# First weight unit of a fused two-block transformer kernel: token loads cut anew, rounding spread over four engines, products reordered

## The reference, cut to what matters

```
h    = concatenate([meta_tokens, x])                  # 528 x 1024
xn   = h * rsqrt(mean(h*h) + 1e-6) * norm_gains[0]
proj = xn @ w_in                                      # q, k, v, forget, gates
```

## Time and profile before

| | us |
|---|---|
| median of 3 runs | 2178.06 |
| lowest, highest | 2177.88, 2178.19 |
| profiled execution, its own time | 2178.15 |
| its span, first to last instruction | 2176.4 |
| PE busy in the span | 2141.2 |
| first product of the unit stream starts | 9.38 |
| sum of squares (after unit 0 and half of unit 1) starts | 29.75 |

### The profile page before, as it was taken

How to read it: one execution, slowest core, us unless ns; L and a number is a source line. 1 busy time by engine, 2 the same in 40 slices (tenths; PEclk the granted TensorE clock), 3 DMA queues, 4 the chain that set the end, 5 groups by cost and what they waited for, 6 DMA issues and landing times.

```text
span 2176.4 us, 31347 instructions
## 1 busy us (share of the span) xinstructions
PE 2141.2 (98%) x12490; PEld 1845.6 (85%) x12490; DVE 996.5 (46%) x1460; ACT 755.3 (35%) x1017; POOL 1008.2 (46%) x825
## 2 busy tenths in 40 slices
PE   8999999999999999999999999999999999999998
PEld 7897999999999887888888788878788888888886
DVE  5144454379888207322200829671876442222027
ACT  4133455243222216322212415551336332222134
POOL 4322223455555547555544545254331555555444
PEclk9999999999999999999999999999999999999999
DMA  4322112212222323322222221114220222222222
GB/s 165 103 69 69 59 45 73 97 59 97 96 85 89 108 96 109 122 96 96 97 97 96 98 105 43 58 58 155 78 78 21 97 97 97 96 96 97 96 100 94
DMA packets 31950, 195.17 MB, mean 90 GB/s; under 512 B 3968, under 2 KB 4480, under 8 KB 10096
## 3 DMA queue, kind: packets, MB, share of 16 engines
q1 hardware_dynamic: 26352, 182.66, 23.4%
q10 hardware_dynamic: 5504, 11.18, 1.7%
HBM read 189.47 MB, written 4.23 MB: 89 GB/s over the span
## 4 chain that ended last, share of the span: by engine, by line
PE 79%; issue 8%; POOL 5%; DVE 5%; ACT 1%; DMA 0%; SPq 0%; DVEq 0%; POOLq 0%; ACTq 0%
PE ps L2370 69%; POOL wlo L708 5%; PE ps L2965 2%; DVE sqa L1520 1%; PE ps L3180 1%; PE ps L3164 1%; PE ps L3047 1%; DVE x2lo L1508 1%; PE ps L3100 1%; PE ps L2649 1%; PE ps L2672 0%; PE ps L3145 0%; PE ps L2708 0%; DMA h<-h 0%; PE ps L3190 0%
## 5 line engine op out<-in xcount | busy, mean ns | idle before, releaser
L708 POOL TENSOR_TENSOR wlo<-raw,whi 128x512 fp32r<-128x512 f32 (+2 forms) x820 | 1006.8, 1260 | 1142.6 <-ACT whi L774 1038.4
L774 ACT CAST whi<-raw 128x2048 fp32r<-128x2048 f32 x162 | 309.6, 1911 | 809.2 <-PE ps L2370 751.9
L2370 PE MATMUL ps<-x2hi,whi 128*128 128x512 f32 x1136 | 448.6, 395 | 1.2 <-DVE x2lo L1508 1.1
L2370 PE MATMUL ps<-x2hi,wlo 128*128 128x512 f32 x1136 | 442.4, 389 | 0.0
L2370 PE MATMUL ps<-x2lo,whi 128*128 128x512 f32 x1136 | 442.2, 389 | 0.0
L2370 PE MATMUL ps<-xhi,whi 128*128 128x256 f32 (+2 forms) x1336 | 270.7, 284 | 15.2 <-DVE xlo L1574 9.4
L2370 PE MATMUL ps<-xlo,whi 128*128 128x256 f32 (+2 forms) x1336 | 268.0, 282 | 0.0
L2370 PE MATMUL ps<-xhi,wlo 128*128 128x256 f32 (+2 forms) x1336 | 268.0, 282 | 0.0
L2370 PEld LDWEIGHTS ps<-x2hi,whi 128*128 128x128 f32 x1136 | 213.3, 188 | 49.6 <-issue 4.8
L2370 PEld LDWEIGHTS ps<-x2hi,wlo 128*128 128x128 f32 x1136 | 213.3, 188 | 44.7
L2370 PEld LDWEIGHTS ps<-x2lo,whi 128*128 128x128 f32 x1136 | 213.4, 188 | 44.4 <-issue 1.7
(11 more groups left out here) (471 smaller groups left out, 2759.8 us busy)
## 6 DMA issues: line engine op xcount, KB each, us to landing
raw<-wstream SPq DMA_DIRECT2D x170, 1024.0 KB, 4.8
h<-h SPq DMA_DIRECT2D x4, 528.0 KB, 8.7
ncb<-c_rows ACTq DMA_DIRECT2D x8, 256.0 KB, 3.4
ple_rows<-ple_out ACTq DMA_DIRECT2D x4, 512.0 KB, 4.1
bias<-bias_rows ACTq DMA_DIRECT2D x8, 256.0 KB, 4.8
ple<-ple_rows ACTq DMA_DIRECT2D x4, 512.0 KB, 5.5
out_dram<-outb SPq DMA_DIRECT2D x8, 256.0 KB, 2.8
raw<-wstream ACTq DMA_DIRECT2D x4, 256.0 KB, 7.3
```

Source lines behind the costliest of these rows:

```text
L708: return nc.gpsimd.tensor_tensor(wlo[b][:, cols], raw[b][:, cols], whi[b][:, cols].bitcast(F32), ALU.subtract)
L774: nc.scalar.copy(whi[b][:], raw[b][:]).then_inc(sig("hi_done"), 1)
L2370: ins = mm(dst, w[slot][:, cols], xx(tok), start=first and p_ == 0, stop=last and p_ == 2, skip_group_check=True)
```

## The change

The gains of the first norm and eight columns of zeros are put in front of the tokens in the same rows (`hg`, 16 + 8 x 528 columns), so the first token transfer brings the gains. SP loads the tokens in five pieces of 1, 1, 1, 2 and 3 chunks, then unit 1, then the three small constants. ACT loads unit 0 as two quarters and a half, and `cv` behind them, and loads its function table ahead of its first wait.

The rounding of unit 0 is spread: ACT rounds quarter 0 and all of `xhi`, POOL copies quarters 1 to 3 to `whi`, DVE makes the four quarters of `wlo` between its eight `xlo`. Unit 1 is rounded by ACT in four quarters, POOL makes its low part, and PE waits for it by quarters.

PE first runs ten products of a zeroed tile (256 columns, fp32) into a bank that is not yet in use, waits for quarter 0, and runs one more. Then it goes over k with the high x high products of chunk k ahead of the other two of chunk k-1.

The diff, cut to its core:

```diff
+HG = 16
...
-    h0 = np.ascontiguousarray(tokens.T.reshape(KC, P, T1).transpose(1, 0, 2))
+    h0 = tokens.T.reshape(KC, P, T1).transpose(1, 0, 2).reshape(P, KC * T1)
+    h0 = np.concatenate([columns(v["norm_gains"][0][0]), np.zeros((P, HG - KC), np.float32), h0], axis=1)
...
-        h = at("h", [P, KC, T1])
+        hg = at("hg", [P, HG + KC * T1])
+        h = hg[:, HG:].rearrange("p (k t) -> p k t", t=T1)
+        x_loads = [(0, 1), (1, 2), (2, 3), (3, 5), (5, KC)]
...
+        idle = at("idle", [P, HALF], offset=arena)
...
-        QUARTERED = [0, U_UP + 1, U_UP + 2, U_PLEP, U_F1I, U_F1I + 1, U_F1I + 2, U_PLEG + 3]
+        QUARTERED = [0, 1, U_UP + 1, U_UP + 2, U_PLEP, U_F1I, U_F1I + 1, U_F1I + 2, U_PLEG + 3]
...
-        HI_FIRST = [0, U_UP + 1, U_UP + 2, U_F1I + 1]
+        HI_FIRST = [0, 1, U_UP + 1, U_UP + 2, U_F1I + 1]
...
-            sp.dma_start(cv[:], cvec).then_inc(sig("gains_in"), 16)
-            for q in range(4):
-                sp.dma_start(h[:, 2 * q:2 * q + 2, :], h0[:, 2 * q:2 * q + 2, :]).then_inc(sig(f"h_in{q}"), 16)
+            for n, (a, z) in enumerate(x_loads):
+                cols = slice(HG + a * T1 if a else 0, HG + z * T1)
+                sp.dma_start(hg[:, cols], h0[:, cols]).then_inc(sig("part_in3" if n == 4 else f"h_in{n}"), 16)
...
+            sp.dma_start(fw0[:], fw).then_inc(sig("consts_in"), 16)
+            sp.dma_start(ident[:], ident_c).then_inc(sig("consts_in"), 16)
+            sp.dma_start(masks[:], masks_c).then_inc(sig("consts_in"), 16)
...
+            for q in range(1, 4):
+                cols = slice(q * BANK, (q + 1) * BANK)
+                if q < 3:
+                    pool.wait_ge(sig(f"part_in{q}"), 16)
+                pool.wait_ge(sig("hi_first"), q)
+                nc.gpsimd.tensor_copy(whi[0][:, cols], raw[0][:, cols]).then_inc(sig("hi_first" if q < 3 else "hi_done"), 1)
+            pool.wait_ge(sig("lo_done"), 1)
...
-                    pool.wait_ge(sig("hi_first"), q + 1)
-                    low_part(0, q).then_inc(sig("lo_first"), 1)
+                    pool.wait_ge(sig("hi_first"), 3 + q + 1)
+                    low_part(1, q).then_inc(sig("lo_first"), 1)
...
-                    pool.wait_ge(sig("hi_done"), 1)
-                    low_part(0, q).then_inc(sig("lo_done"), 1)
-            pool.wait_ge(sig("hi_done"), 2)
-            for q in range(3):
-                low_part(1, q)
-            low_part(1, 3).then_inc(sig("lo_done"), 1)
+                    pool.wait_ge(sig("hi_done"), 2)
+                    low_part(1, q).then_inc(sig("lo_done"), 1)
...
+            act.dma_start(raw[0][:, 0:BANK], wstream[0][:, 0:BANK]).then_inc(sig("part_in0"), 16)
+            act.dma_start(raw[0][:, BANK:2 * BANK], wstream[0][:, BANK:2 * BANK]).then_inc(sig("part_in1"), 16)
+            act.dma_start(raw[0][:, 2 * BANK:], wstream[0][:, 2 * BANK:]).then_inc(sig("part_in2"), 16)
+            act.dma_start(cv[:], cvec).then_inc(sig("gains_in"), 16)
+            nc.scalar.preload_act_table_set("natural_log_exp_and_others")
+            act.wait_ge(sig("part_in0"), 16)
+            nc.scalar.copy(whi[0][:, 0:BANK], raw[0][:, 0:BANK]).then_inc(sig("hi_first"), 1)
+            for n, (a, z) in enumerate(x_loads):
+                act.wait_ge(sig("part_in3" if n == 4 else f"h_in{n}"), 16)
+                for k in range(a, z):
+                    nc.scalar.activation(xhi[:, k, :], h[:, k, :], ACT.Copy, scale=hg[:, k:k + 1]
+                                         ).then_inc(sig("xhi_ready"), 1)
+            act.wait_ge(sig("hi_done"), 1)
+            act.wait_ge(sig("raw_ready1"), 16)
+            act.wait_ge(sig("hi_first"), 3)
...
-                act.dma_start(raw[0][:, q * BANK:(q + 1) * BANK], wstream[0][:, q * BANK:(q + 1) * BANK]
-                              ).then_inc(sig(f"part_in{q}"), 16)
-            act.dma_start(fw0[:], fw).then_inc(sig("fw_in"), 16)
-            act.dma_start(ident[:], ident_c).then_inc(sig("ident_in"), 16)
-            act.dma_start(masks[:], masks_c).then_inc(sig("masks_in"), 16)
-            act.wait_ge(sig("gains_in"), 16)
-            for q in range(4):
-                act.wait_ge(sig(f"part_in{q}"), 16)
...
-                nc.scalar.copy(whi[0][:, cols], raw[0][:, cols]).then_inc(sig("hi_first" if q < 3 else "hi_done"), 1)
-                act.wait_ge(sig(f"h_in{q}"), 16)
-                for k in (2 * q, 2 * q + 1):
-                    nc.scalar.activation(xhi[:, k, :], h[:, k, :], ACT.Copy, scale=cv[:, G_PRE + k:G_PRE + k + 1]
-                                         ).then_inc(sig("xhi_ready"), 1)
-            hi_of(1)
-            nc.scalar.preload_act_table_set("natural_log_exp_and_others")
+                nc.scalar.copy(whi[1][:, cols], raw[1][:, cols]).then_inc(sig("hi_first" if q < 3 else "hi_done"), 1)
...
-            act.wait_ge(sig("fw_in"), 16)
+            act.wait_ge(sig("consts_in"), 48)
+            act.wait_ge(sig("gains_in"), 16)
...
-            act.wait_ge(sig("ident_in"), 16)
-            act.wait_ge(sig("masks_in"), 16)
...
+            vec.memset(idle[:], 0.0).then_inc(sig("cols_ready"), 1)
...
-            dve.wait_ge(sig("gains_in"), 16)
...
+                if k % 2 == 0:
+                    q, cols = k // 2, slice(k * HALF, k * HALF + BANK)
+                    dve.wait_ge(sig("hi_first" if q < 3 else "hi_done"), q + 1 if q < 3 else 1)
+                    vec.tensor_tensor(wlo[0][:, cols], raw[0][:, cols], whi[0][:, cols].bitcast(F32), ALU.subtract
+                                      ).then_inc(sig("lo_first" if q < 3 else "lo_done"), 1)
...
-                vec.scalar_tensor_tensor(out=xlo[:, k, :], in0=h[:, k, :], scalar=cv[:, G_PRE + k:G_PRE + k + 1],
+                vec.scalar_tensor_tensor(out=xlo[:, k, :], in0=h[:, k, :], scalar=hg[:, k:k + 1],
...
+            dve.wait_ge(sig("gains_in"), 16)
...
+            def idle_turns(n):
+                for _ in range(n):
+                    mm(bank(7)[:, 0:HALF], idle[:, 0:P], idle[:], start=True, stop=True)
+            def high_tile(k, c):
+                for dst, tok in wide_places(STAGE1[c]):
+                    ins = mm(dst, whi[0][:, (2 * k + c) * P:(2 * k + c + 1) * P], xhi[:, k, tok], start=k == 0,
+                             stop=False, skip_group_check=True)
+                return ins
+            def low_tile(k, c):
+                cols = slice((2 * k + c) * P, (2 * k + c + 1) * P)
+                for w, xx, last in ((whi, xlo, False), (wlo, xhi, k == KC - 1)):
+                    for dst, tok in wide_places(STAGE1[c]):
+                        ins = mm(dst, w[0][:, cols], xx[:, k, tok], start=False, stop=last, skip_group_check=True)
+                return ins
+            pe.wait_ge(sig("cols_ready"), 1)
+            idle_turns(10)
+            pe.wait_ge(sig("hi_first"), 1)
+            idle_turns(1)
+            for k in range(KC + 1):
+                if k < KC:
+                    if k % 2 == 0:
+                        pe.wait_ge(sig("hi_first" if k < 6 else "hi_done"), k // 2 + 1 if k < 6 else 1)
+                    pe.wait_ge(sig("xhi_ready"), k + 1)
+                    for c in range(2):
+                        high_tile(k, c)
+                if k >= 1:
+                    if k % 2 == 1:
+                        low_ready(0, k // 2)
+                    pe.wait_ge(sig("x_ready"), k)
+                    for c in range(2):
+                        ins = low_tile(k - 1, c)
+                        if k == KC:
+                            ins.then_inc(sig("unit_done" if c else "half"), 1)
...
-                    if k < 6:
-                        pe.wait_ge(sig("lo_first"), k // 2 + 1)
-                    else:
-                        pe.wait_ge(sig("lo_done"), 1)
-                pe.wait_ge(sig("x_ready"), k + 1)
-                ins = chunk_tile(0, 0, k, STAGE1[0])
-                if k == KC - 1:
-                    ins.then_inc(sig("half"), 1)
-                ins = chunk_tile(0, 1, k, STAGE1[1])
-            ins.then_inc(sig("unit_done"), 1)
-            pe.wait_ge(sig("lo_done"), 2)
-            chunk(1, 0, 2)
-            pe.wait_ge(sig("cols_ready"), 1)
+                    low_ready(1, k // 2)
+                ins = chunk_tile(1, 0, k, STAGE1[2])
+            ins.then_inc(sig("half"), 1)
+            pe.wait_ge(sig("cols_ready"), 2)
```

## The result

| | before | after |
|---|---|---|
| median, us | 2177.97 (4 runs, 2177.88 to 2178.19) | 2190.97 (4 runs, 2190.36 to 2192.56) |
| ratio of times | | 1.0061 (95% interval 1.0049 to 1.0073) |
| span of the profiled execution, us | 2176.4 | 2188.7 |
| sum of squares starts, us | 29.75 | 26.54 |
| from there to the end, us | 2146.61 | 2162.16 |

The change made the kernel 13.0 us slower, where 3.8 us faster was forecast. The last two lines say where: up to the sum of squares 3.2 us were gained, and behind it, in code that the change does not touch, 15.5 us were lost.

What follows compares the result with a forecast made beforehand. PE, busy 98% of the span, was taken as the bound; 1.5 us by earlier S, 2.0 by the clock and 0.62 by the gap, less 0.5 of stalls, gave 3.8 us gained: 2174.3 us, range 2173.3 to 2176.6.

Steps and rivals of the forecast that it cites:

- Everything behind 29.75: All work from the sum of squares on: taken to move along whole, so its start, 29.75 us before, measures the change.
- the last, that later stages lose: Rival, behind the start: the start moves and later stages wait for something else instead; chance 0.04.
- S = 7.86: Start of PE's first real product, after idle products from 1.17 us: 4.0 us slow, then 2.69 us fast.
- Idle products of zeros don't raise the clock: Rival, PE's start: idle work leaves the clock slow, S = 10.55, kernel at 2178.4 us; chance 0.06.
- The fast pace: PE's early products: 0.122 us each at 2.4 GHz, 17.57 us for unit 0 and unit 1's first chunk.
- Landings: Token transfers at the start: chunk 2 lands at 9.32 us, chunks 3 and 4 at 10.96, chunks 5 to 7 at 12.9.
- Small pieces: Rival, first transfers: small pieces come at 291 GB/s, 2.9 us gained, kernel at 2175.1 us; chance 0.12.
- ACT's table load ahead of the wait: ACT's start: the 1.28 us table load is hidden behind the transfer, ending near 4.1 us.
- POOL copy, 1.3 us: POOL's copies of unit 0's quarters 1 to 3: 1.3 us each, hidden even at 1.85.
- DVE as the bound: Rival, unit 0's low parts: DVE slowed beside POOL ends 1.6 us late, kernel at 2175.9 us; chance 0.10.
- The squares, 0 to 0.3 us late: DVE's adds of squares ahead of the sum: end near 25.3 to 26.2, wanted at 25.94; taken as 0.
- 2.0 us by the clock: PE's first real products: 2.0 us gained because idle products raise the clock before them.

Runs made afterwards that it cites:

- b1_pad64: The kernel before with 64 unused bytes behind the tokens and no instruction changed: 2193.17 us, ratio 1.0069 to the kernel before.
- a_gap256: The changed kernel with 192 more unused bytes behind the tokens, 256 bytes of added distance in all: 2174.99 us, ratio 0.9988 to the kernel before.
- a_gap512: The changed kernel with 448 more unused bytes behind the tokens, 512 bytes of added distance in all: 2175.47 us, ratio 0.9989 to the kernel before.
- best_x0: `a_gap256` in the old product order, with output-stage and first feed-forward inputs 0 instead of 8 columns into their rows: 2177.86 us, ratio 1.0000 to before.
- a_noidle: `a_gap256` without its eleven idle products: 2175.37 us, ratio 0.9988 to the kernel before.
- a2_tail64: The changed kernel with 64 unused bytes behind the tokens, everything behind them 128 bytes further than before the change: 2211.22 us, ratio 1.0157 to before.

## Why the prediction was wrong

The step that failed is the one the sum rested on: "Everything behind 29.75 is released by PE's own progress or by ACT and DVE steps that start from it. I take it to move along whole". The releases did move along whole. What I did not ask is whether the work behind keeps its pace. It did not: 64 bytes more ahead of the token-side buffers cost 2.2 ns on each product of 512 columns and somewhat on shorter ones, 15.5 us together (`b1_pad64`: 15.4 alone). The kernel has some 6000 products of 512 columns, by estimate 13 of the 15.5 us; the products of 256 and 258 columns have most of the rest. The edit that did it stood in the diff as a layout detail, `hg` in place of `h`, and I priced it at nothing without naming it. None of the rivals had it; the last, that later stages lose, was there with a chance of 0.04 and the wrong mechanism.

The rest, point by point:

- *S = 7.86.* Real products began at 8.10. The idle pitch halved 4.7 us after the first idle product, not 4.0; in `a_gap256` 6.0 us after, and S was 8.74. The term was right in kind and 0.2 to 0.9 us too small.
- *Idle products of zeros don't raise the clock.* They do: records 427 ns apart turn into records 216 ns apart before any real product has run.
- *The fast pace.* 0.122 us a product stood beside a row that gives 4.0/34 = 0.118, because the row counts products cut by the window's edges too. After the change a pair takes 0.243 us in the timeline, so 0.122 was right.
- *Landings.* The count of bytes that must come first gave 9.32, 10.96 and 12.9; ACT could start at 9.58, 11.22 and 13.13. Small pieces were not slow.
- *ACT's table load ahead of the wait.* It lies at 3.11 to 4.39, hidden.
- *POOL copy, 1.3 us.* It took 0.87 and hid as forecast:

```profile
L724 POOL CAST whi<-raw 128x512 fp32r<-128x512 f32 x3 | 2.6, 874 | 8.5 <-DMA raw<-wstream 8.5
```

- *DVE as the bound.* No: its last `xlo` of unit 0 ended at 16.7.
- *The squares, 0 to 0.3 us late.* 0.16 us in the changed kernel, 0 (`a_gap512`) to 0.61 (`best_x0`) in those at 256 or 512 bytes.
- *2.0 us by the clock.* This was no gain on top of the earlier inputs. `a_noidle` has the slow start still and its median is 0.4 us above that of `a_gap256`, less than the runs can tell; in the profiles its sum of squares starts 0.1 us behind that of `a_gap256` and 0.8 behind that of the changed kernel. With the tokens as late as they are, the two terms overlap; my sum counted them apart and took only 0.5 us of stalls off.
- *The start in sum.* 3.8 us forecast, 3.2 measured, and 2.9 at the end of the kernel once the distance is a multiple of 256 bytes again.

## What to carry to other kernels

Ask of every edit which buffers it moves, and compare the pitch of an untouched product deep in the kernel before anything else: a count of products in one window that PE fills shows in a minute what no list of waits does. When a buffer grows, keep the distance between the matrices loaded as weights and those that move past them at the multiple of 256 bytes it had, here by 192 unused bytes. That is shown for fp32r products of 512 columns only; for pairs of 256 and 258 columns it was not the best place. A gain of some us at the start is lost easily to a percent of pace behind it.

## What the runs showed of the hardware

- The pace of an fp32r product of 512 columns depends on the distance, modulo 256 bytes, between its moving operand and the weight tiles: 226.7 ns at 0, 228.9 at 64, 231.8 to 234.4 at eight other places. In this kernel that is 15 us at 64 bytes, and at 32 or 128 it is 33 to 34 us against the kernel before and 36 to 37 against `a_gap256`. The granted clock is 1.00 from 900 to 1000 us and from 470 to 2160 us in all of them. It falls near 450 us in each of these kernels: between 440 and 465 its mean is 0.86 in the kernel before, the changed one, `b1_pad64` and `a_gap256`, and 0.80 in the kernels at 32, 128 and 384 bytes. So it has no part in the 15 us, and in the 33 to 37 at most 1.5 (an estimate, 0.06 of 25 us). The Trainium skill (TensorE: Matmul & The Clock Gate, "Step-by-step: what each phase is for") says that PE has two independent read ports and that loading the next tile's weights takes nothing from the running product. The measurement decides, and it differs: on zeros, with no other engine at those buffers, the same loads and products take 3% longer when only the distance between the two operands changes. What in PE collides is not shown.
- The point at which the pace rose after PE's first work moved from kernel to kernel: 4.1 us after it in the kernel before and 5.4 in `b1_pad64`, which runs the same instructions; with idle products 3.0 in `a2_tail64`, 4.7 in the changed kernel, 6.0 and 6.4 in `a_gap256` and `a_gap512`. `a_gap256`, whose first product comes at 1.2 us, scatters more from run to run (2174.01 to 2177.70) than the kernel before beside it (2176.81 to 2178.48); that the moving point is the cause was not tried.
- The records of the plain fp32 idle products stand 216 ns apart at the fast pace for 256 columns.
